# Constant products in TensorE's waits, low halves kept in the ring, and a new order at four hand-overs

## The chip, the cores and the metric

The kernel runs on one core of a Trainium2 chip. The metric is the device time of one execution in microseconds (us). A core has five engines that run their own instruction streams and wait for each other through semaphores: TensorE (PE in the profile; PEld are its weight loads), VectorE (DVE), ScalarE (ACT), GpSimd (POOL) and SyncE (SP), which here only issues DMAs.

## What is computed

One inference step of a hybrid backbone with two layers, on 128 context tokens and 256 latent tokens of width 1024 (384 tokens together). Cut to what matters:

```python
def _layer(x, mod, lp, router_w, router_b, rope, ctx_kv, h0):
    sh1, sc1, g1, sh2, sc2, g2 = mod          # Linear(SiLU(cond)), 6 x 1024 columns
    h = _rmsnorm(x, lp['norm1']) * (1 + sc1) + sh1
    q, k, v, xr, gr, ga, gb = jnp.split(h @ lp['w_in'], IN_SPLITS, axis=-1)
    att = ...                                 # grouped-query attention, 8 heads, 2 kv heads
    rnn, h_last = _rglru_bidir(xr, lp, h0)    # conv, gates, two scans
    merged = (jax.nn.sigmoid(ga) * (att @ lp['w_attn_proj'])
              + jax.nn.sigmoid(gb) * ((jax.nn.gelu(gr) * rnn) @ lp['w_rnn_proj']))
    x = x + g1 * (merged @ lp['w_out'])
    h2 = _rmsnorm(x, lp['norm2']) * (1 + sc2) + sh2
    x = x + g2 * _moe(h2, router_w, router_b, lp['w_gate_up'], lp['w_down'])
    return x, k, v, h_last
```

`_moe` routes each token to 2 of 16 experts (SwiGLU, inner width 512). After the second layer there is a last RMSNorm. All is fp32.

## The kernel before

**Precision.** Most products are made from two halves in the faster fp32r type: a high half (the rounded value) and a low half (value minus high half). ScalarE makes the high half of a weight tile (`high_part`, line 1031; `piece_high`, line 1226), VectorE the low half (`low_part`, line 1497; `piece_low`, line 1838), and TensorE adds high x high, high x low and low x high (`split_product`, line 522; `split_piece`, lines 820 and 826).

**Weights.** SyncE streams them in an order fixed by `chunk_order`. Chunks of 2 MB (1024 rows x 512 columns) go into a `ring` of three slots; the experts' pieces of 1 MB go into eight `spots`, six of which lie over the ring and two over `parts`. Before each load SyncE waits for the release of what was in the place (`released`): for a chunk whose products are split that is the last low half made of it. SyncE's queue is in order. Split products in order are q, xr, gr (the first 24, `EARLY`), then ap, rp, wo (the late 24); each has 8 column tiles of 128, four to a chunk. High and low halves of a tile go into one of three pairs of places (`w_parts`); for the late ones these lie in `hT`, `spare` and `xc`. `AHEAD` is 2: the halves of tile n + 2 are asked for when product n is due.

**The order in a layer.** TensorE: h products for k, v (`product`, line 511); split products q and xr; 24 attention units, each with scores, a product of gr, ga or gb, the turn of the probabilities, the two gate products of one recurrent pair from unit 8 on, and `attend` (line 685) of the unit before; then ap, rp, wo; squares for the norm; the router's logits (line 744); transposes of the rows (line 752); `rank` (line 772), `ids` (line 779), the gates (line 784); the turn of the first expert's rows (`xturn`, line 792) and 16 experts, each with four pieces of gate-up and two of down. ScalarE and VectorE follow the order of their own streams, written out by hand:

- End of attention. In unit 23 ScalarE runs `exps`, `lru_root(14)`, the tanh of gb, `pt_copy(23)`, `lru_tables(15)` (lines 1124 to 1134), `att_copy(22)` (line 1110), and behind the loop `lru_root(15)` (line 1140), `high_part(24)`, `att_copy(23)`, `high_part(25)`. VectorE runs `one_minus_square(15)`, `low_part(24)`, `att_split(7)`, `low_part(25)`, `scan(15)`. The last `attend` waits for `att_copy(22)`; product ap0 waits for its low half and `att_split(7)`.
- Experts. The results of experts 0 to 13 are stored to memory (`store_y`, line 1255) and gathered by token by GpSimd (line 1997) into `yg`; those of 14 and 15 are held on the chip and spread by a selection matrix (line 895). ScalarE scales the rows (line 1266), VectorE combines them (line 1893) and makes the low halves of the held ones (line 1888); TensorE transposes the rows (`rows_in`, line 890), adds the held ones, and VectorE adds the sums to x (`add_group`, line 1901, semaphore `group_added`).
- `one_more`. A branch that each engine takes by the number of further blocks (0 with these inputs) follows; the count is read by `value_load`. ScalarE asks for the Sqrt table by a one-column activation (line 1297) ahead of it.
- Into the next layer. SyncE issues kv, q0 and ada4 of layer 1 when the gathers are back. ScalarE squares x (line 1327), TensorE sums the squares with a matrix of ones (line 548), ScalarE takes the root (line 1005), VectorE the reciprocal (line 1461) and the product with x (line 1468), GpSimd (line 1965) and ScalarE (line 1041) apply the modulation, and product k0 starts. After layer 1 the rows are turned (line 951), squared (line 1332), rooted (line 1343), scaled (line 1947) and stored.

## Time and profile before

| | us |
|---|---|
| median of 3 runs (lowest, highest) | 1584.49 (1583.61, 1587.31) |
| the profiled execution, whole | 1587.41 |
| its span, first to last instruction | 1585.5 |
| TensorE busy | 1485.0 (94%) |
| VectorE busy | 1116.2 (70%) |
| ScalarE busy | 926.0 (58%) |
| mean granted TensorE clock | 0.967 |

Times in the rows are microseconds from the first instruction of the profiled execution. Busy time is the union of an engine's instructions. Matmul records overlap, their ends are modelled. The granted clock is 1.00 at 2.4 GHz and 0.50 at 1.2 GHz. What stands in square brackets at the end of a row is the idle time of the engine before it and what ended it; "issue" means that the profile shows no releaser.

### The profile page before, as it was taken

What the parts mean: (1) busy time and instruction counts of PE and PEld (TensorE: products, weight loads), DVE (VectorE), ACT (ScalarE), POOL (GpSimd) and SP (SyncE); (2) the same over time, 40 slices, a digit from 0 to 9 for tenths busy, and PEclk for the clock granted to TensorE, in tenths of its full rate; (3) what the DMA queues carried; (4) which work ended last, traced back from release to release, by engine and by line L of the source; (5) the groups of instructions that cost most, each with busy time, mean ns of one, the idle gap of its engine ahead of it and who ended that gap; (6) DMA issues with size and microseconds to landing.
All of it is one profiled execution on the core that took longest, in us unless ns stands there. A gap on an engine that the chain in (4) does not pass through costs nothing.

```text
span 1585.5 us, 19352 instructions
## 1 busy us (share of the span) xinstructions
PE 1485.0 (94%) x7317; PEld 1195.4 (75%) x7317; DVE 1116.2 (70%) x1709; ACT 926.0 (58%) x1174; POOL 153.3 (10%) x209
## 2 busy tenths in 40 slices
PE   6999999989996999999979999999899599999996
PEld 3699866669875788888748998665898378888885
DVE  4447656765646999999852665776564689999996
ACT  1333579962224877778742245899321467787874
POOL 0100012200010000000230000221000200000002
PEclk8999999989997999999989999999899699999999
DMA  9455422124656999999744554112340789999993
GB/s 349 163 199 203 153 103 101 62 102 166 212 193 253 358 406 408 409 408 404 278 162 154 186 199 161 62 62 90 128 160 1 279 311 407 413 411 410 408 357 121
DMA packets 132708, 373.01 MB, mean 235 GB/s; under 512 B 9216, under 2 KB 12672, under 8 KB 132608
## 3 DMA queue, kind: packets, MB, share of 16 engines
q1 hardware_dynamic: 113728, 326.57, 54.9%
q0 software_dynamic: 10432, 25.18, 4.5%
q10 hardware_dynamic: 8448, 19.94, 3.2%
q8 instruction: 63, 1.03, 0.3%
q14 instruction: 37, 0.30, 0.1%
HBM read 351.71 MB, written 19.94 MB: 234 GB/s over the span
## 4 chain that ended last, share of the span: by engine, by line
PE 79%; DVE 7%; ACT 4%; issue 4%; DMA 4%; POOL 1%; SPq 0%; POOLq 0%; DVEq 0%; ACTq 0%
PE bank L522 24%; PE bank L820 19%; PE bank L511 10%; PE bank L826 10%; PE bank L532 2%; PE bank L712 2%; PE bank L792 2%; DMA ring<-in_w_ada 1%; PE bank L685 1%; PE bank L548 1%; DMA expert_rows<-gb 1%; PE bank L541 1%; PE bank L622 1%; PE bank L617 1%; DMA tmp<-expert_rows,posu 1%
## 5 line engine op out<-in xcount | busy, mean ns | idle before, releaser
L1838 DVE TENSOR_TENSOR spot_low<-spot,piece_high 128x2048 fp32r<-128x2048 f32 x192 | 434.1, 2287 | 32.8 <-ACT piece_high L1226 31.5
L1226 ACT ACTIVATE piece_high<-spot 128x2048 fp32r<-128x2048 f32 x192 | 366.9, 1917 | 46.6 <-PE bank L826 45.4
L820 PE MATMUL bank<-piece_high,ga_r 128*128 128x512 f32 x768 | 310.9, 405 | 4.7 <-ACT ga_r L1231 2.2
L820 PE MATMUL bank<-spot_low,ga_r 128*128 128x512 f32 x768 | 303.7, 395 | 0.0
L826 PE MATMUL bank<-piece_high,ga_r 128*128 128x512 f32 x768 | 211.6, 397 | 0.0
L511 PE MATMUL bank<-hT,ring 128*128 128x384 f32 x576 | 198.0, 499 | 9.6 <-ACT hT L1041 6.5
L522 PE MATMUL bank<-parts_r,ga_r 128*128 128x384 f32 x768 | 202.6, 345 | 0.0
L820 PEld LDWEIGHTS bank<-piece_high,ga_r 128*128 128x128 f32 x768 | 145.6, 190 | 39.0 <-ACT ga_r L1231 3.0
L511 PEld LDWEIGHTS bank<-hT,ring 128*128 128x128 f32 x576 | 109.2, 195 | 82.6 <-issue 11.3
L826 PEld LDWEIGHTS bank<-piece_high,ga_r 128*128 128x128 f32 x768 | 145.1, 189 | 34.8
L820 PEld LDWEIGHTS bank<-spot_low,ga_r 128*128 128x128 f32 x768 | 145.9, 190 | 31.0
L522 PEld LDWEIGHTS bank<-parts_r,ga_r 128*128 128x128 f32 x768 | 138.3, 188 | 5.9 <-issue 5.0
L522 PE MATMUL bank<-parts_r,gb_r 128*128 128x384 f32 x384 | 129.7, 338 | 0.0
L522 PE MATMUL bank<-parts_r,hT_r 128*128 128x384 f32 x432 | 99.0, 356 | 9.1 <-DVE parts_r L1489 9.1
L522 PEld LDWEIGHTS bank<-parts_r,hT_r 128*128 128x128 f32 x432 | 81.3, 199 | 12.8 <-DVE parts_r L1489 10.9
L1497 DVE TENSOR_TENSOR gb_r<-ring,ga_r 128x1024 fp32r<-128x1024 f32 x48 | 58.5, 1222 | 44.1 <-ACT ga_r L1031 42.4
L1984 POOL DMA_INDIRECT gr<-h_rows,ids x32 | 44.0, 1375 | 464.0 <-PE bank L792 429.7
L1977 POOL DMA_DIRECT2D gatew<-in_lru_wa x64 | 34.2, 539 | 473.5 <-PE bank L712 473.5
L1031 ACT ACTIVATE hT_r<-ring 128x1024 fp32r<-128x1024 f32 x32 | 33.9, 1058 | 78.0 <-PE bank L522 78.0
L522 PEld LDWEIGHTS bank<-parts_r,gb_r 128*128 128x128 f32 x384 | 72.1, 188 | 0.0
L1001 ACT ACTIVATE tmp<-bank 128x512 f32<-128x512 f32 x24 | 14.3, 598 | 75.9 <-PE bank L532 75.9
L1965 POOL TENSOR_SCALAR hT<-hT,modA,modT 128x128 f32<-128x128 f32 x32 | 23.4, 745 | 361.6 <-DVE hT L1468 322.4
(308 smaller groups left out, 2289.3 us busy)
## 6 DMA issues: line engine op xcount, KB each, us to landing
spot<-in_w_gate_up SPq DMA_DIRECT2D x128, 1024.0 KB, 8.0
spot<-in_w_down SPq DMA_DIRECT2D x64, 1024.0 KB, 8.3
ring<-in_w_ada SPq DMA_DIRECT2D x24, 2048.0 KB, 8.0
ring<-in_w_in SPq DMA_DIRECT2D x22, 2048.0 KB, 8.0
expert_rows<-gb ACTq DMA_DIRECT2D x28, 512.0 KB, 7.3
ring<-in_w_attn_proj SPq DMA_DIRECT2D x4, 2048.0 KB, 8.6
ring<-in_w_rnn_proj SPq DMA_DIRECT2D x4, 2048.0 KB, 8.3
ring<-in_w_out SPq DMA_DIRECT2D x4, 2048.0 KB, 8.0
```

What stands on the lines that cost most here:

```text
L511: mm = pe.matmul(bank[:, 0:width], slot_kn(slot)[:, k, n * P:(n + 1) * P], rhs(k), start=(k == 0), stop=(k == KT - 1))
L522: mm = pe.matmul(bank[:, 0:T], w[:, k, :], x[:, k, :], start=(k == 0 and i == 0), stop=(k == KT - 1 and i == 2))
L532: mm = pe.matmul(bank[g:g + 32, :], cpad[:, k, :], slot_kn(s)[:, k, :], start=(k < 4), stop=(k >= 4), tile_position=(0, g))
L712: pe.matmul(bank[:, 0:CW], gatew[:, which, n % 2, :], xc[:, j, :], start=True, stop=True).then_inc(S("gemm_done"), 1)
L820: pe.matmul(out[n], high[:, 2 * q + k, :], w[:, k, n * 512:(n + 1) * 512], start=(q == 0 and k == 0 and i == 0), stop=False)
L826: mm = pe.matmul(out[n], low[:, 2 * q + k, :], w_high[:, k, n * 512:(n + 1) * 512], start=False, stop=(q == pieces - 1 and k == 1))
L1031: ac.activation(w_part(kind, n)[0], slot_kn(s)[:, :, n % 4 * P:(n % 4 + 1) * P], ACT.Copy)\
L1226: ac.activation(highs[p % HIGHS], spots[u], ACT.Copy).then_inc(S("piece_high"), 1)
L1497: ve.tensor_tensor(low, slot_kn(s)[:, :, n % 4 * P:(n % 4 + 1) * P], high.bitcast(F32), ALU.subtract)\
L1838: ve.tensor_tensor(spots_low[u], spots[u], highs[p % HIGHS].bitcast(F32), ALU.subtract)\
L1977: po.dma_start(gatew[half * 64:half * 64 + 64, which, n % 2, half * 64:half * 64 + 64], w[l, d, 2 * j + half]).then_inc(S(f"gatew_loaded{n ...
L1984: po.indirect_dma_start(out=dst, out_offset=None, in_=h2d[:, :], in_offset=bass.IndirectOffsetOnAxis(ap=idx, axis=0)).then_inc(sem, 16)
```

## The change

What it does, in the order of the diff:

1. High halves of late tiles go round four places (`late_high`: `spare` and three in `hT`), and their low halves are written over the tile itself in the ring slot (`w_low_part`). A late chunk is therefore released by its fourth product (`gemm_done`) and not by its last low half. `xc` is no longer a place for halves.
2. SyncE waits ahead of layer 1's kv chunk until all of layer 0's groups are added.
3. `run_on` gives TensorE products of `ident` and constants into a bank that nobody reads: two of 384 columns ahead of `rank`, four of 512 ahead of `ids`, three ahead of the first `xturn` and one behind it, three ahead of `rows_in`, six behind the square sums at the end of layer 0.
4. End of attention: `high_part(24)` goes behind `exps(23)`, and `lru_tables(15)`, `one_minus_square(15)` and `lru_root(15)` go behind `att_copy(23)` and the halves of tile 25.
5. In the last expert ScalarE copies and stores the result of expert 13 ahead of the last gate-up piece.
6. The activation that asks for the Sqrt table goes behind `one_more`.
7. VectorE makes the low halves of the held results between the combinations of rows and not behind them.

```diff
+LATE_HIGHS = 4
-        w_parts = [[(part(gaf_r, i), part(gbf_r, i)) for i in range(PAIRS_OF_PARTS)],
-                   [(part(hTf, 0), part(hTf, 1)), (part(hTf, 2), part(spare_r, 0)), (part(xcf, 0), part(xcf, 1))]]
+        w_parts = [(part(gaf_r, i), part(gbf_r, i)) for i in range(PAIRS_OF_PARTS)]
+        late_high = [part(spare_r, 0)] + [part(hTf, i) for i in range(LATE_HIGHS - 1)]
+        ring_r = sb_r("ring")
...
+        def w_high_part(kind, n):
             at = SPLIT_AT[kind, n]
+            return w_parts[at % PAIRS_OF_PARTS][0] if at < EARLY else late_high[at % LATE_HIGHS]
+        def w_low_part(l, kind, n):
+            at = SPLIT_AT[kind, n]
+            if at < EARLY:
+                return w_parts[at % PAIRS_OF_PARTS][1]
+            s = CHUNK_SLOT[CHUNK_AT[(l, f"{kind}{n // 4}")]][0]
+            return ring_r[:, s, :].rearrange("p (k n) -> p k n", k=KT)[:, :, n % 4 * P:(n % 4 + 1) * P]
...
-                if g[1:] in SPLIT_AT:
+                if SPLIT_AT.get(g[1:], EARLY) < EARLY:
                     return S("w_low"), split_no(*g) + 1
...
+                if l and name == "kv":
+                    sy.wait_ge(S("group_added"), l * KT)
...
+            def run_on(bank, times, width=512):
+                for _ in range(times):
+                    pe.matmul(bank[:, 0:width], ident, con[:, 256:256 + width], start=True, stop=True)
...
+                run_on(SB[1], 2, T)
                 bank = t_take((l, "rank", 0))
...
+                run_on(SB[1], 4)
                 bank = t_take((l, "ids", 0))
...
+                run_on(SB[1], 3)
                 xturn(0)
+                run_on(SB[1], 1)
...
+                run_on(G[2], 3)
                 for g in range(6):
                     rows_in(g)
...
                     mm.then_inc(S("ss_done"), 1)
+                    run_on(G[2], 6)
                     continue
...
-                    nth = at % EARLY
-                    if nth >= PAIRS_OF_PARTS:
+                    if at >= EARLY + LATE_HIGHS:
+                        ac.wait_ge(S("gemm_done"), G_AT[(l, *SPLIT[at - LATE_HIGHS])] + 1)
+                    elif at > EARLY:
+                        ac.wait_ge(S("gemm_done"), G_AT[(l, "gb", KT - 1)] + 1)
+                    elif PAIRS_OF_PARTS <= at < EARLY:
                         ac.wait_ge(S("gemm_done"), G_AT[(l, *SPLIT[at - PAIRS_OF_PARTS])] + 1)
-                    elif at >= EARLY:
-                        ac.wait_ge(S("gemm_done"), G_AT[(l, "gb", KT - 1)] + 1)
-                        if nth == 2:
-                            ac.wait_ge(S("lru_used"), (l + 1) * 16)
...
                     exps(i)
+                    if i == 3 * KT - 1:
+                        high_part(EARLY)
...
-                    if i >= KT:
+                    if KT <= i < 3 * KT - 1:
                         lru_tables(i - KT)
                     if i >= 1:
                         att_copy(i - 1)
-                lru_root(15)
-                high_part(EARLY)
                 att_copy(23)
                 high_part(EARLY + 1)
+                lru_tables(15)
+                lru_root(15)
...
-                    piece_high(f"gu{e}", 3)
+                    if e < NE - 1:
+                        piece_high(f"gu{e}", 3)
                     if e >= 2:
                         copy_y(e - 2)
+                    if e == NE - 1:
+                        store_y(e - 2)
+                        piece_high(f"gu{e}", 3)
...
-                ac.activation(smx[:, 0, 7:8], ones[:, 0:1], ACT.Sqrt)
...
                 one_more(0)
+                ac.activation(smx[:, 0, 7:8], ones[:, 0:1], ACT.Sqrt)
...
-                one_minus_square(15)
                 low_part(EARLY)
                 att_split(HEADS - 1)
                 low_part(EARLY + 1)
+                one_minus_square(15)
                 scan(15)
...
-                for i in range(HELD):
-                    ve.wait_ge(S("y_copied"), l * NE + SENT + i + 1)
-                    low_of(i, (SB_pair, G_pair)[i], slot_gate[:, SENT + i:SENT + i + 1]).then_inc(S("held_low"), 1)
+                    if t:
+                        i = t - 1
+                        ve.wait_ge(S("y_copied"), l * NE + SENT + i + 1)
+                        low_of(i, (SB_pair, G_pair)[i], slot_gate[:, SENT + i:SENT + i + 1]).then_inc(S("held_low"), 1)
```

## Rows read from the trace of the kernel before

**Rows 1.** The page: busy time by engine, and one of its costliest groups.

```profile
PE 1485.0 (94%) x7317; PEld 1195.4 (75%) x7317; DVE 1116.2 (70%) x1709; ACT 926.0 (58%) x1174; POOL 153.3 (10%) x209
...
L820 PE MATMUL bank<-spot_low,ga_r 128*128 128x512 f32 x768 | 303.7, 395 | 0.0
```

**Rows 2.** Windows: stretch, length, busy time of each engine, granted clock, DMA share, GB/s.

```profile
336.00:346.00 10.00, 6.32 (x21) 6.05 (x22) 7.19 (x15) 4.21 (x7) 0.00 (x0) 0.50 0.18 66
483.00:503.00 20.00, 11.58 (x39) 9.93 (x40) 14.32 (x27) 5.63 (x5) 2.96 (x3) 0.50 0.45 160
817.50:824.00 6.50, 5.43 (x9) 2.82 (x10) 5.48 (x8) 5.28 (x9) 6.50 (x6) 0.50 0.00 1
1251.00:1271.00 20.00, 9.84 (x43) 8.61 (x44) 14.75 (x40) 8.33 (x5) 2.97 (x3) 0.50 0.56 211
```

**Rows 3.** Timeline of TensorE in the routing: start, length, engine, line, operation.

```profile
487.29 1.42 PE L779 MATMUL bank<-gb_r 128*128 128x22 f32 x6 [5.48 <-DVE gb_r L1789]
...
494.31 1.97 PE L792 MATMUL bank<-con,gr 128*128 128x128 f32 x8 [3.02 <-DMA gr<-h_rows,ids]
497.39 0.79 PE L820 MATMUL bank<-piece_high,ga_r 128*128 128x512 f32 x1 [1.11 <-ACT ga_r L1231]
...
511.31 1.03 PE L792 MATMUL bank<-con,gr 128*128 128x128 f32 x8
...
1267.52 0.79 PE L820 MATMUL bank<-piece_high,ga_r 128*128 128x512 f32 x1 [1.11 <-ACT ga_r L1231]
```

**Rows 4.** Timeline of TensorE at the end of layer 0's attention.

```profile
336.49 1.20 PE L685 MATMUL bank<-pt,vl 128*128 128x128 f32 x4 [3.56 <-ACT qT L1110]
...
341.31 7.06 PE L522 MATMUL bank<-parts_r,hT_r 128*128 128x384 f32 x26 [3.19 <-DVE parts_r L1489]
```

**Rows 5.** Timeline of TensorE at the layers' ends and into layer 1.

```profile
795.98 0.41 PE L895 MATMUL bank<-qT_r,gb_r 128*128 128x384 f32 x1 [0.23 <-DVE gr_r L1888]
...
805.92 7.12 PE L548 MATMUL bank<-hT,ones 128*128 128x384 f32 x16 [3.42 <-issue]
818.57 13.33 PE L511 MATMUL bank<-hT,ring 128*128 128x384 f32 x32 [5.52 <-ACT hT L1041]
831.74 7.03 PE L617 MATMUL bank<-ring,hT 128*128 128x512 f32 x16
...
1572.27 2.84 PE L951 MATMUL bank<-con,xT 128*128 128x128 f32 x24 [0.58 <-issue]
```

**Rows 6.** Timeline of ScalarE at the end of layer 0's attention.

```profile
333.37 0.59 ACT L1124 ACTIVATE tmp<-bank,hb 128x387 f32<-128x387 f32 x1
...
336.09 0.26 ACT L1110 ACTIVATE qT<-bank 128x128 f32<-128x128 f32 x1
...
338.09 1.04 ACT L1031 ACTIVATE hT_r<-ring 128x1024 fp32r<-128x1024 f32 x1
339.04 0.26 ACT L1110 ACTIVATE qT<-bank 128x128 f32<-128x128 f32 x1
```

**Rows 7.** Timeline of VectorE, the last operation of scan(15).

```profile
346.38 0.56 DVE L1489 TENSOR_TENSOR gr_r<-gr,qT_r 128x384 fp32r<-128x384 f32 x1
```

**Rows 8.** The tile ring, issued between 790 and 792 us: kv and q0.

```profile
DMA to landing us min/median/max: 8.0/11.0/13.9
```

**Rows 9.** DMA queues between 803.2 and 804 us, and between 1569.7 and 1570.

```profile
q1 hardware_dynamic: 154, 0.29, 96.0%
q8 instruction: 1, 0.02, 8.2%
...
q8 instruction: 1, 0.02, 20.9%
```

**Rows 10.** Timeline of GpSimd, the modulation of the context tokens in layer 1.

```profile
816.93 8.07 POOL L1965 TENSOR_SCALAR hT<-hT,modA,modT 128x128 f32<-128x128 f32 x8 [30.07 <-DVE hT L1468]
```

**Rows 11.** Waits of TensorE over the span: us in total, times, longest.

```profile
PE bank L890 <- DVE tmp L1893: 4.0, 2, 2.0
```

**Rows 12.** Timeline of ScalarE at the end of layer 1.

```profile
1576.69 1.28 ACT L1343 ACT_TABLE_LOAD   x1
...
1578.19 0.58 ACT L1332 ACTIVATE hT<-bank 128x512 f32<-128x512 f32 x1
```

10 lines of the change are left out of this document (4 added, 6 removed).

## The prediction

> **What bounds the kernel now.** I read the page first: TensorE is busy for 94% of the span [rows 1], so a gain has to come out of its idle gaps or out of stretches in which its products run slowly. The table of windows gives the second kind: in three kinds of place the granted clock is at 0.50, the 1.2 GHz level [rows 2]: at the end of attention, in the routing, and on either side of the step from layer 0 to layer 1. Each of them follows a gap of TensorE. The reader should see in the timeline that the products of one and the same form take twice as long there: eight transposes 1.97 us against 1.03 [rows 3]. So a gap is paid twice, once as a wait and once as slow products behind it, and I went through the gaps with the timeline of each engine and the chain of waits. They are: the end of attention, 3.56 and 3.19 us [rows 4]; the routing, waits until 487.29, 494.31 and 497.39 us [rows 3]; the end of a layer, until 805.92 and 818.57 us [rows 5].
>
> **The change, part by part.**
>
> **1. End of attention, twice.** Before the last `attend`, TensorE waits for `att_copy(22)` at 336.09 us, which ScalarE issues behind `lru_tables(15)`; that takes from 333.37 to 336.09, 2.72 us [rows 6]. The change moves `lru_tables(15)` behind, and puts `high_part(24)`, 1.04 us [rows 6], ahead. So `att_copy(22)` starts at 336.09 - 2.72 + 1.04 = 334.41, and the last `attend` 1.68 us earlier, at 334.8. It takes 1.6 us, 1.20 of them in its first group of products [rows 4], the cached values behind it. `att_copy(23)` no longer stands behind `lru_root(15)` and `high_part(24)`: it comes at 336.45 in place of 339.04 [rows 6]. VectorE then needs only `att_split(7)`, two operations of about 1 us together, so product ap0 starts at about 337.75 and not at 341.31 [rows 4]: 3.5 us. What is late next is the low half for ap2: in VectorE's queue it stands behind `scan(15)`, which now ends near 346.5 (it was 346.94 [rows 7], and its root comes later relative to ap0). That half would be ready near 347.7. ap0 and ap1 still run partly at 0.50, since TensorE is idle here for over 3 us all the same, and ap1 ends after 348, so nothing waits; were the clock up, ap2 would wait and the gain would stop at about 4.3. I take 3.5 for each layer, 7.0 in all, bounds 6 and 8.6.
>
> **2. High halves in four places, low halves in the ring.** The weight slot is now free when the fourth product of a chunk is done and not when its low half is made, some 8 us (two products) later. A chunk lands 8.0 us after its issue when nothing is ahead of it [rows 8], and the products that need it come more than that later; SyncE's queue is in order, but the chunks behind wait for modulation products anyway. I cost it at nothing; if the cover were gone it would be up to 8 us at each of five chunks, which is the bound I do not take.
>
> **3. Constant products in the routing, twice.** One 512-column product costs 7.03 / 8 = 0.88 us at the full clock [rows 5], a 384-column one about three quarters, 0.66. Two of the latter go ahead of `rank`, four of 0.88 (3.5 us) ahead of `ids`, three (2.6 us) ahead of the turn of the first rows, one behind. `ids` starts at 487.29 after 5.48 us of idling, the turn after 3.02, gate-up after 1.11 [rows 3]: each fits while the clock is up. What they give: `ids` costs 1.42 us at the low level, so 0.7 less, of which 0.6 reaches the gather; the turn 1.97 down to 1.03, 0.9 less; and from 497.39 to the end of the low stretch at 503, 5.6 us at half rate, 2.8 less [rows 2, 3]. Layer 0: 4.3 us. In layer 1 the first piece starts at 1267.52 and the low stretch ends at 1271 [rows 2, 3], 1.8 us in place of 2.8: 3.3 us. Sum 7.6 us. The bounds are 8.5 and, should the dummies start at the low level, about -3 (the second rival). What hides behind: VectorE needs 4.5 us for the first two low halves and they begin earlier too.
>
> **4. Layer 0 to layer 1.** (a) Between the last product of the layer, 802.5, and the first square sum at 805.92 the profile names no releaser for 3.42 us [rows 5]. There stands the branch of `one_more`. An instruction transfer of 16 KB starts between 803.2 and 804, in a stretch that the three weight chunks issued from 791.1 on fill; in layer 1 the same branch costs 0.58 us [rows 5], and the like transfer starts between 1569.7 and 1570 with nothing else moving [rows 9]. TensorE goes on some 2.4 us after either. So I read the 3.42 as a code fetch behind 6 MB of weights. The change holds these loads back until `group_added` is complete, one addition after TensorE's last product, near 803.3, and TensorE has its code by then: the gap falls to 0.6, 2.8 us less. The squares, 7.12 us at a clock that falls on the way [rows 5], take 8 x 0.65 = 5.2 at the full one: 1.9 less. (b) The chunks now land 8.0 us and more after 803.4, kv at 811.5, where its first product comes at 813.8 at the earliest; q0 and ada4 (in the row the second of two lands after 13.9 us [rows 8]) are needed only some 12 us after that product. SyncE has nothing else queued behind. No cost. (c) Six dummies, 5.3 us, stand in the wait of 5.52 us for the normalised rows [rows 5]: they fit, and the first product runs at the full clock. GpSimd paces it, though: its eight pieces end at 825.0 [rows 10], so that of the time lost at the low level only about 1.2 us comes back. (a) and (c): 6.0 us, bounds 2.5 and 6.5.
>
> **5. Rows of the experts, twice.** `store_y(13)` goes ahead of one high half, so the rows may come back earlier; one low half of the held experts slips into the wait for the last rows. Together they could take away the idle 2.0 us ahead of the transposes [rows 11] and the 0.23 ahead of the spread at 795.98 [rows 5]. But three dummies, 2.6 us, now stand in that place, and TensorE runs them whatever has arrived. The transposes then start 0.5 us later, 0.2 of it stood as the wait ahead of the spread, and pauses between the two may hold some more: I cost the whole at 0.1 us lost, twice, bounds -0.3 and 0.6. Here the change gives back what it gained.
>
> **6. ScalarE's table for Sqrt.** It is asked for behind the branch and not ahead of it. In layer 1 a table load of 1.28 us stands at 1576.69, in series with the end, and after the Sqrt behind it Square runs at 1578.19 with no load of its own [rows 12]: one table serves both, and the load comes only because the branch hides which one is in. Behind the branch it is loaded in ScalarE's wait: 1.3 us less; everything behind it is in series. In layer 0 the load is hidden. The Trainium skill, page "ScalarE: Activation LUTs", section "What ACT_TABLE_LOAD costs", puts a switch at some 2.7 us with a drain; the Square at 1578.19, with the Sqrt before it, starts 1.5 us after the load does, so the trace does not agree; by the page the sum would be 1.4 us lower.
>
> **The sum.** 7.0 + 7.6 + 6.0 + 1.3 - 0.2 = 21.7 us. The profiled execution took 1587.4 us with a span of 1585.5, so it would take 1565.7. The median of the runs shown, 1584.5, is 2.9 below it: 1562.8, rounded to 1563.
>
> **The rivals.** First, the gap at 802.5 is the price of the taken branch itself and not of the loads. Against it: 0.58 us in layer 1. For it: layer 1 may have had its code by chance of position, and the change shifts positions. Then the 3.4 us and the slow squares stay: 1563 + 4.7 = 1568. The Trainium skill, page "Runtime: NRT & Kernel Launch", section "Instruction fetch mechanics", states such a rule: a taken branch whose target is not held stalls until the code is fetched. The trace agrees that there is a fetch, and leaves open what its length hangs on. Second, the dummies do not keep the clock up in the routing. For it: gaps of nearly 2 us remain between them, and `ids` and the gates have only 22 columns. Then the four ahead of `ids` last 7.0 us and end 1.6 late, the three ahead of the turn 5.3 and end 3.6 late in all, the one behind it adds 0.6; what follows has the full clock, 2.8 back. That is 1.4 lost for each layer in place of 3.8 gained: 1563 + 10.4 = 1573. It is also the case in which the change does not do what it says. Third, slower than before: low halves in the ring slot make the 48 late products slower, by TensorE reading weights from the slot that VectorE writes next to. The price is 48 times what each grows by; it decides from 25 / 48 = 0.5 us, a ninth of a product. Against it: the expert stage does the same in place, and its products on fresh low halves take 395 ns with no idling before them [rows 1]. With 0.6 us each the kernel would take about 1592.
>
> **How the numbers follow.** My forecast has 0.62, with a range of its own from 1558 to 1568. The branch has 0.14, the clock 0.18, the slower products 0.03, and 0.03 is left for small mishaps that eat everything. The range from 1558 (all upper bounds) to 1573 takes in the first three, but for the tails. A measurement here tells 0.2%, 3 us, from no change. Faster by more: 0.94; within: 0.03; slower: 0.03.
>
> **What would show it.** ap0 should start some 3.5 us earlier against the last `attend` but one; the granted clock should read 1.00 when gate-up begins, in both layers; the gap before the square sums should be under 1 us and the squares 5.2 us; the spread should start no earlier than now against the last down product; no table load at the second Sqrt. Wrong would be a wait of TensorE behind a run of dummies, a first product of layer 1 that waits for `ring`, or products of ap, rp and wo above 4.2 us.

## The result and the profile after

The changed kernel takes 1566.58 us (median of four executions, 1566.03 to 1567.22), where the kernel before takes 1584.05 (1583.37 to 1587.31): a ratio of 0.9886, 95% interval 0.9869 to 0.9903. The profiled execution took 1566.03 us with a span of 1564.2. The forecast was 1563, so it was 3.6 us too low, inside its range. One execution of this study, of the kernel without constant products in the routing, ran in a slow state (1888.3 us at a mean granted clock of 0.744) and is left out of its median.

Table of windows of the changed kernel; the columns are those of [rows 2].

```profile
334.00:340.00 6.00, 5.26 (x16) 5.27 (x17) 3.58 (x7) 5.94 (x9) 0.00 (x0) 0.50 0.25 89
484.00:487.00 3.00, 3.00 (x5) 1.12 (x4) 3.00 (x2) 0.00 (x0) 2.47 (x2) 0.50 0.52 173
487.40:800.00 312.60, 308.17 (x1428) 248.91 (x1427) 276.65 (x212) 232.68 (x171) 29.86 (x20) 1.00 0.95 367
800.00:1217.00 417.00, 402.16 (x2039) 325.15 (x2038) 249.73 (x532) 209.34 (x385) 41.67 (x72) 1.00 0.35 124
```

The column ahead of the DMA share, the granted clock, tells the story: of the 20 us at 0.50 in each routing [rows 2] about 3.4 are left, and between 487 and 1217 us the clock doesn't fall at all, neither at the step between the layers nor at the end of layer 1's attention. TensorE's timeline at the places of [rows 3], [rows 4] and [rows 5]:

```profile
332.48 0.68 PE L702 MATMUL bank<-pt,vl 128*128 128x128 f32 x4 [1.78 <-ACT qT L1132]
334.74 1.01 PE L539 MATMUL bank<-parts_r,spare_r 128*128 128x384 f32 x2 [1.35 <-DVE parts_r L1517]
...
481.36 0.81 PE L798 MATMUL bank<-gb_r 128*128 128x22 f32 x6 [1.95 <-DVE gb_r L1817]
...
483.36 4.52 PE L514 MATMUL bank<-con 128*128 128x512 f32 x6
487.72 1.04 PE L811 MATMUL bank<-con,gr 128*128 128x128 f32 x8
...
489.87 0.50 PE L839 MATMUL bank<-piece_high,ga_r 128*128 128x512 f32 x1 [0.25 <-ACT ga_r L1255]
...
784.76 0.30 PE L911 MATMUL bank<-con,gb 128*128 128x128 f32 x1 [0.75 <-DVE tmp L1921]
...
794.14 5.43 PE L565 MATMUL bank<-hT,ones 128*128 128x384 f32 x16 [0.93 <-ACT hT L1355]
799.41 5.31 PE L514 MATMUL bank<-con 128*128 128x512 f32 x12
805.10 0.88 PE L528 MATMUL bank<-hT,ring 128*128 128x384 f32 x2 [0.37 <-ACT hT L1063]
806.39 3.30 PE L528 MATMUL bank<-hT,ring 128*128 128x384 f32 x8 [0.41 <-POOL hT L1994]
810.70 7.36 PE L528 MATMUL bank<-hT,ring 128*128 128x384 f32 x22 [1.01 <-POOL hT L1994]
```

L514 is `run_on`, the constant products. The wait ahead of the last `attend` went from 3.56 to 1.78 us and the one ahead of ap0 from 3.19 to 1.35 [rows 4]; the idle time ahead of the square sums from 3.42 to 0.93 (what ends it now is a square of ScalarE, L1355), and the squares from 7.12 to 5.43 us [rows 5]; the turn from 1.97 to 1.04 [rows 3].

To see where the time went I subtract the start of the same instruction in the two profiled executions, place by place; what the difference grows by in a stretch is what that stretch gave. The sum is the 21.3 us between the two spans.

| stretch | forecast | layer 0 | layer 1 |
|---|---|---|---|
| up to the first query projection of layer 0 | 0 | 2.2 | |
| from there to ap2 (attention and its end) | 3.5 each | 4.0 | 5.7 |
| late products, up to the logits' end | 0 | -0.3 | -0.1 |
| routing, up to the first activation turn | 4.3 and 3.3 | 4.3 | 2.5 |
| last activation turn to the spread (rows) | -0.1 each | -0.9 | -1.4 |
| spread's end to layer 1's first query projection | 6.0 | 4.5 | |
| spread's end to the end | 1.3 | | 0.9 |

"Spread's end" here and below is the start of its last product. Two things must be known to read the table. The first row is not the change's: what is done up to there is the same, and the first query projection starts between 68.2 and 71.3 us in the profiles of this study (the kernel before, 70.75), with the clock low in other stretches of the first 50 us each time. And the profiled execution of the kernel before was 3.4 us above its median while that of the changed one was 0.6 below: 21.3 less 3.4 and less 0.6 is about the 17.5 between the medians.

### The profile page after: what moved, and what is told of

It is laid out like the page before. It is cut to its first block, busy times and chain, and to the rows that moved or that the text cites. A ratio compares the mean times of both kernels' runs of the same rounds, so it can differ in the third digit from the quotient of the medians.

```text
span 1564.2 us, 19475 instructions
## 1 busy us (share of the span) xinstructions
PE 1496.1 (96%) x7381; PEld 1192.7 (76%) x7381; DVE 1115.0 (71%) x1709; ACT 919.3 (59%) x1170; POOL 157.8 (10%) x209
## 4 chain that ended last, share of the span: by engine, by line
PE 78%; DVE 7%; ACT 4%; DMA 4%; issue 4%; POOL 2%; SPq 0%; POOLq 0%; DVEq 0%; ACTq 0%
PE bank L539 23%; PE bank L839 19%; PE bank L528 10%; PE bank L845 10%; PE bank L549 2%; DMA ring<-in_w_ada 2%; PE bank L729 2%; PE bank L811 2%; PE bank L702 1%; PE bank L565 1%; DMA expert_rows<-gb 1%; PE bank L639 1%; PE bank L634 1%; PE bank L558 1%; DMA ring<-in_w_out 1%
## 5 line engine op out<-in xcount | busy, mean ns | idle before, releaser
L539 PE MATMUL bank<-parts_r,ring_r 128*128 128x384 f32 x256 | 86.8, 339 | 0.0
L539 PEld LDWEIGHTS bank<-parts_r,hT_r 128*128 128x128 f32 x384 | 69.3, 188 | 3.8 <-DVE ring_r L1525 1.4
L1053 ACT ACTIVATE hT_r<-ring 128x1024 fp32r<-128x1024 f32 x36 | 37.1, 1053 | 37.7 <-PE bank L539 37.7
## 6 DMA issues: line engine op xcount, KB each, us to landing
ring<-in_w_rnn_proj SPq DMA_DIRECT2D x4, 2048.0 KB, 10.3
```

Of the source, the lines that this page charges most:

```text
L539: mm = pe.matmul(bank[:, 0:T], w[:, k, :], x[:, k, :], start=(k == 0 and i == 0), stop=(k == KT - 1 and i == 2))
L1053: ac.activation(w_high_part(kind, n), slot_kn(s)[:, :, n % 4 * P:(n % 4 + 1) * P], ACT.Copy)\
```

## The experiments

Executions of one and the same kernel lie up to 7 us apart here (the kernel before, 1580.92 to 1588.11 in one session). Between the profiles of the study the clock falls or doesn't in half a dozen short waits, each worth 1 to 1.5 us, and that is the likely reason. The changed kernel and its variants ran in different sessions, in which the kernel before had medians from 1582.94 to 1584.36. So I read each edit first in its own stretch of the profile, and the median second. Each kernel has one profile.

### The step from layer 0 to layer 1

**Without SyncE's wait.**

```diff
-                if l and name == "kv":
-                    sy.wait_ge(S("group_added"), l * KT)
```

> The changed kernel without the wait that SyncE holds ahead of layer 1's first query chunk; all else as changed. Theory A (the idle time ahead of the square sums is the fetch of the branch's code, and its length hangs on the weight transfers that run beside it): the gap ahead of the square sums returns from 0.93 us to about 3.4, the granted clock falls behind it, the squares take about 7 us and not 5.43; from the last product of layer 0 to the first of layer 1 the kernel loses 2.5 to 4.5 us, and the whole takes about 1569 to 1571 us. Theory B (the branch has its own price, and the shorter gap comes from the position of the code): the gap stays below 1.5 us and the time at 1566.6.

Measured: 1571.57 us, ratio 0.9925 (0.9906 to 0.9944) to the kernel before. TensorE's timeline and the DMA queues in the idle time:

```profile
798.80 5.51 PE L563 MATMUL bank<-hT,ones 128*128 128x384 f32 x11 [3.38 <-issue]
804.52 1.88 PE L563 MATMUL bank<-hT,ones 128*128 128x384 f32 x5 [0.21 <-issue]
...
q1 hardware_dynamic: 728, 1.46, 103.3%
q8 instruction: 1, 0.02, 1.7%
```

The stretch from the spread's end to the first query projection takes 43.25 us, as in the kernel before (43.16), where the changed one takes 38.61: the wait alone is worth the whole 4.6 us. The median is 5.0 above the changed kernel's, 0.6 more than the upper end of A. The squares start at the full clock and fall into a stretch at 0.50 from 800.0 to 803.4 us. The queues show what is different: in the 3.8 us up to the squares the weights (q1) fill the sixteen engines, one instruction transfer (q8) between them. In the changed kernel the queues' view of the gap, from 792.9 to 795.0 us, holds two instruction transfers and no weights; one of them:

```profile
q8 instruction: 1, 0.02, 3.3%
```

Theory A holds; the first rival of the forecast (the branch's own price) falls, since both kernels take the same branch. The Trainium skill, page "Runtime: NRT & Kernel Launch", section "Instruction fetch mechanics", has a taken branch wait for the fetch of its page; that there is such a wait agrees, with at most 0.5 to 1.0 us of idling in the twelve other profiles that have SyncE's wait, and 3.4 where weights move.

**Without the six constant products.**

```diff
                     mm.then_inc(S("ss_done"), 1)
-                    run_on(G[2], 6)
```

> The changed kernel without the six constant products in the wait for layer 1's first normalised rows. Theory A (GpSimd's pieces pace the first product, so that the clock there is worth little): the first product starts at the low level and the kernel loses 0.3 to 1.0 us: 1567 to 1567.6. Theory B (my forecast's term, 1.2 us, and the key and value product behind it also at the low level): 1567.8 or more. Theory C (the six end later than the rows are there): it gains up to 0.4 us.

Measured: 1564.72 us, 0.9883 (0.9860 to 0.9906).

```profile
805.81 5.30 PE L528 MATMUL bank<-hT,ring 128*128 128x384 f32 x10 [5.53 <-ACT hT L1062]
811.41 7.36 PE L528 MATMUL bank<-hT,ring 128*128 128x384 f32 x22 [0.30 <-POOL hT L1993]
...
804.17 8.05 POOL L1993 TENSOR_SCALAR hT<-hT,modA,modT 128x128 f32<-128x128 f32 x8 [25.14 <-DVE hT L1495]
```

The first ten products now run at 0.50, 5.30 us for what took 3.30 + 0.88 with waits of 0.41 and 1.01 between; and the key and value product behind them starts 14.44 us after GpSimd's first piece, exactly as in the changed kernel. So the six are worth nothing here: GpSimd's eight pieces, 8.05 us, set the pace at either clock. From the spread's end to the first query projection it takes 38.14 us; the other kernels with SyncE's wait take 38.15 to 38.66. All three theories gave them some price and all three were wrong in size; the idea of A (GpSimd paces it) holds, with 0 in place of 0.3 to 1.0. That the median is 1.9 us below the changed kernel's I don't count: the profiled execution was 1.0 above that of the changed kernel.

### The rows of the experts

**The old order of the store.**

```diff
-                    if e < NE - 1:
-                        piece_high(f"gu{e}", 3)
+                    piece_high(f"gu{e}", 3)
                     if e >= 2:
                         copy_y(e - 2)
-                    if e == NE - 1:
-                        store_y(e - 2)
-                        piece_high(f"gu{e}", 3)
                     if e >= 1:
                         piece_high(f"dn{e - 1}", 0)
-                    if 2 <= e < NE - 1:
+                    if e >= 2:
                         store_y(e - 2)
```

> The changed kernel with the old order of the store of the last but two expert's rows (one high half ahead of it again). Theory A (the last rows come late because GpSimd's gather calls start some 0.4 us later against VectorE's large operations and one of them then waits for such an operation's end; the earlier store runs under weight transfers and lands no earlier): the last gathered rows land 1 to 2 us earlier against the first turn of the rows, and the stretch from the last turn to the spread takes up to that much less in both layers: 1564.5 to 1566. Theory B (the dummies ahead of the rows set the start of the transposes, as my forecast said): nothing changes or it loses 0.2 us; 1566.6. The third case, the earlier store does help: the rows land 1.8 us later, 1568 or more.

Measured: 1564.61 us, 0.9885 (0.9865 to 0.9906). From the last activation turn to the spread it takes 11.41 and 11.43 us; the changed kernel takes 12.36 and 12.94, the kernel before 11.48 and 11.54. So with the old order 2.4 us less are spent here in the two layers. GpSimd's six calls that gather the rows back, and VectorE beside them, in layer 0 of the changed kernel (start, length):

```profile
766.42 2.76 POOL L2026 DMA_INDIRECT hT<-expert_rows,posu  x1 [49.37 <-issue]
...
771.98 2.49 POOL L2026 DMA_INDIRECT qT<-expert_rows,posu  x1 [0.30 <-issue]
774.77 1.89 POOL L2026 DMA_INDIRECT tmp<-expert_rows,posu  x1 [0.30 <-issue]
776.97 0.94 POOL L2026 DMA_INDIRECT tmp<-expert_rows,posu  x1 [0.30 <-issue]
...
761.67 6.70 DVE L1866 TENSOR_TENSOR spot_low<-spot,piece_high 128x2048 fp32r<-128x2048 f32 x3 [1.84 <-ACT piece_high L1250]
...
771.36 4.50 DVE L1866 TENSOR_TENSOR spot_low<-spot,piece_high 128x2048 fp32r<-128x2048 f32 x2 [0.40 <-ACT piece_high L1250]
```

and of this run:

```profile
764.20 1.03 POOL L2022 DMA_INDIRECT hT<-expert_rows,posu  x1 [47.92 <-issue]
765.53 2.15 POOL L2022 DMA_INDIRECT gb<-expert_rows,posu  x1 [0.30 <-issue]
...
770.47 0.94 POOL L2022 DMA_INDIRECT tmp<-expert_rows,posu  x1 [0.30 <-issue]
771.71 1.98 POOL L2022 DMA_INDIRECT tmp<-expert_rows,posu  x1 [0.31 <-issue]
```

A call that VectorE leaves alone takes 0.94 us. One that meets a low half, 2.29 us on VectorE, ends 0.81 us after that low half does: in the changed kernel the first at 769.18 (the third low half of the group ends at 768.37) and the fourth at 774.47 (VectorE's operation ends at 773.66). The changed order makes the high half of `gu15.3` later; its low half and the two behind it now run in one block, and the third ends 0.7 us later against the last turn. So the first call ends 0.7 us later too (-5.1 us, not -5.9), and the fourth, which had slipped in just ahead of the next low half, is caught by it. The sixth then ends 3.6 us behind the last turn, one place later than the 2.4 of the kernel before. (In this run it ends 0.15 us behind in layer 0 and 2.35 in layer 1; the constant products hold the spread at 11.4 either way.)

The earlier issue gave nothing back: against the last turn the store is issued at -15.0 in place of -13.2 us, and lands at -8.6 (6.4 us later) in place of -9.0 (4.2 later), while weight transfers still run.

The new order does not cost this every time. The first call starts 0.7 us after the last store has landed. Of the 16 layers profiled with the new order and whole low halves, in 13 the store lands 8.9 us or less ahead of the last turn, the third low half catches the first call, and the sixth ends 3.6 us behind the turn. In the other three (both layers of the kernel with two constant products ahead of the turn, further down, and layer 0 of the one without any in the routing) it landed 9.1 to 10.0 us ahead: the first call started 8.4 to 9.3 us ahead and was over before the third low half could hold it up, the sixth ended at 2.35, and the spread started at 11.4 as with the old order. One of them, the first two calls, 7.3 and 5.1 us ahead of the turn at their ends:

```profile
766.51 1.19 POOL L2026 DMA_INDIRECT hT<-expert_rows,posu  x1 [48.73 <-issue]
768.01 1.90 POOL L2026 DMA_INDIRECT gb<-expert_rows,posu  x1 [0.30 <-issue]
```

In none of the six layers with the old order and whole low halves did a sixth call end later than 2.4. The cost of the order is thus 0.9 to 2.0 us in a layer where the store lands too late for the first call to be over before the third low half, as in 13 of 16, and nothing in the others.

**The low halves in two.** This tests the mechanism by itself, with the new order kept.

```diff
-                    ve.tensor_tensor(spots_low[u], spots[u], highs[p % HIGHS].bitcast(F32), ALU.subtract)\
-                        .then_inc(S("piece_low"), 1)
+                    if name in (f"dn{NE - 2}", f"gu{NE - 1}", f"dn{NE - 1}"):
+                        ve.tensor_tensor(spots_low[u][:, 0:1024], spots[u][:, 0:1024],
+                                         highs[p % HIGHS].bitcast(F32)[:, 0:1024], ALU.subtract)
...
```

> The changed kernel with the low halves of the last weight chunks of the expert stage (the last one of gate-up of the last expert, and those of the last two down projections) made by VectorE as two operations of 128x1024 each in place of one of 128x2048. Theory A (a row-gather call of GpSimd that meets a running low-half operation completes only 0.8 us after that operation ends): the calls that stand beside them shrink from 2.5 and 1.9 us to 1 to 1.9 us, the sixth call ends 1 us or more earlier against the first turn of the rows than the 3.59 us of the changed kernel, and the stretch to the spread gives back up to 1 us in each layer: 1564.6 to 1566. Theory B (the calls are long for a reason of their own, such as the descriptors or the transfers): the calls keep their times and nothing changes, 1566.6.

Measured: 1565.09 us, 0.9887 (0.9863 to 0.9910); last turn to spread 11.41 us in both layers.

```profile
772.43 0.94 POOL L2033 DMA_INDIRECT tmp<-expert_rows,posu  x1 [0.30 <-issue]
773.67 1.11 POOL L2033 DMA_INDIRECT tmp<-expert_rows,posu  x1 [0.30 <-issue]
...
772.74 1.23 DVE L1867 TENSOR_TENSOR spot_low<-spot,piece_high 128x1024 fp32r<-128x1024 f32 x1 [0.40 <-ACT piece_high L1250]
```

The sixth call meets the first half operation (until 773.97) and ends at 774.78, again 0.81 us after it; it takes 1.11 us. In layer 1 it ends 1.35 us after the last turn and not 3.6. Theory A holds: what a gather call waits for is the end of VectorE's operation, whether that takes 2.29 or 1.23 us. The Trainium skill, page "SBUF — State Buffer", section "SBUF: two separate sides", has a rule that fits: VectorE, with two operands in SBUF, and GpSimd share a pair of ports that one holds for a whole instruction. The calls' waits fit it. That the lock is held for a whole instruction does not show on VectorE's side: its next low half starts right behind the one that a call waited for and keeps its 2.29 us while that call runs. No run shows that it is this pair of ports and nothing else that they wait for.

**Without the three constant products ahead of the rows.**

```diff
-                run_on(G[2], 3)
                 for g in range(6):
                     rows_in(g)
```

> The changed kernel without the three constant products ahead of the transposes of the experts' rows. Theory A (the rows themselves are late, the dummies stand in a wait that is there anyway): 1566.6 within 0.5 us, with the transposes starting no earlier; if the clock falls in that gap, up to 1 us more for each layer. Theory B (my forecast: the dummies are what the transposes wait for): the transposes start 0.5 us earlier or more in each layer, 1565 to 1565.6.

Measured: 1570.60 us, 0.9912 (0.9889 to 0.9935). TensorE's first transpose of layer 0, and the window behind it:

```profile
787.68 0.45 PE L911 MATMUL bank<-con,gb 128*128 128x128 f32 x1 [3.38 <-DVE tmp L1920]
...
787.50:790.50 3.00, 2.82 (x14) 2.85 (x15) 1.23 (x2) 1.23 (x2) 0.00 (x0) 0.50 1.02 398
```

TensorE idles 3.38 us in layer 0 and 2.76 in layer 1, the clock falls behind both, and from the last turn to the spread it takes 13.86 and 13.04 us (12.36 and 12.94 in the changed kernel, whose last rows in layer 1 landed 1.1 us later). The transposes start 2.6 us after the last rows have landed in all four of these layers, with the dummies (landed 7.81 us after the last turn, start at 10.44) and without (7.86 and 10.49). In the changed kernel, then, the rows are what is late and the dummies cost nothing, as A has it with its price for the clock; my forecast's reason (they are what the transposes wait for) is wrong for the kernel as it is. The median is 4.0 us above the changed kernel's and A allowed 2.5: the stretches hold 1.6, and the profiled execution lost 2.8 more before layer 0's first query projection and 1.5 behind the wait for layer 1's wo0, where the clock fell.

**The same with the rows on time:** the old order of the store and no dummies.

> The changed kernel with the old order of the last store of rows and without the three constant products ahead of the transposes of these rows. Theory A (with the rows on time the dummies, 2.7 us, are what the transposes wait for, as my forecast priced them): the spread starts earlier against the last turn than the 11.41 us of the run with the old order and the dummies, by up to 0.6 us in each layer. Theory B (with the rows on time TensorE's wait is over 2 us with or without them, and the clock falls or not by chance): the spread starts at 11.41 to 11.5 us, or 1 to 1.5 later in a layer in which the clock falls. Time: 1563.5 to 1564.6 by A, 1564.6 to 1567 by B.

Measured: 1564.53 us, 0.9874 (0.9850 to 0.9898); last turn to spread 10.69 and 10.24 us, where the old order with the dummies has 11.41 and 11.43.

```profile
785.71 0.30 PE L911 MATMUL bank<-con,gb 128*128 128x128 f32 x1 [1.66 <-DVE tmp L1916]
...
1542.62 0.30 PE L911 MATMUL bank<-con,gb 128*128 128x128 f32 x1 [1.19 <-DVE tmp L1916]
```

So with the rows on time the dummies do hold the transposes back, by 0.7 and 1.2 us, and behind the waits without them, 1.66 and 1.19 us, the clock did not fall. Both readings were right, each in its own case. Layer 0 also bears on the moved low half of the held experts: 10.69 us against 11.48 in the kernel before, with the same order of the store. 0.3 of this is that the last rows landed 0.3 us earlier; from the first transpose to the spread it takes 1.91 in place of 2.39 us, and that 0.5 is what the moved low half can be worth. It was not undone alone.

**Old order and short low halves.**

> The changed kernel with two repairs: the old order of the last store of rows, and the low halves of the last chunks in two operations each. If both act on the same thing (the time of the sixth gather call against VectorE's low halves), they do not add: each alone brought the spread to 11.41 us after the last turn, and so do both: 2.4 us less than the changed kernel in the two layers, 1564.2, with the sixth call ended before 1.4 us after the last turn in both layers. If they add, the spread starts before 11.2 us and the time is 1563.5 or less.

Measured: 1566.37 us, 0.9888 (0.9864 to 0.9912), last turn to spread 11.41 us in both layers: they do not add, as one would think of two remedies for one thing; TensorE's dummies are the next limit. The time itself is 2 us above what I gave. In the profile the 2.4 us are there; 2.0 are lost ahead of layer 0's first query projection and 1.3 at the end of layer 1's attention, where the clock fell for 6.8 us in this execution and not in the changed kernel's.

**All three repairs.**

> The changed kernel with three repairs: the old order of the last store of rows, the low halves of the last chunks in two operations each, and no constant products ahead of the transposes of the rows. Theory A (the rows come on time by the first two, and the dummies are then what the transposes wait for): the spread starts 10.2 to 10.7 us after the last turn in both layers, where the changed kernel has 12.36 and 12.94, so 4.0 to 4.9 us less in the two layers and a time of 1561.7 to 1562.6. Theory B (the clock falls in the wait without the dummies, as it did once in the run that had only them taken out): 1 to 1.5 us of that is lost again in one layer or both, 1562.6 to 1565.

Measured: 1561.72 us (1560.32 to 1564.32), 0.9865 (0.9847 to 0.9883), last turn to spread 10.24 us in both layers, 2.1 and 2.7 less than in the changed kernel.

```profile
773.84 1.97 POOL L2028 DMA_INDIRECT tmp<-expert_rows,posu  x1 [0.30 <-issue]
...
782.78 0.30 PE L911 MATMUL bank<-con,gb 128*128 128x128 f32 x1 [1.20 <-DVE tmp L1923]
```

Theory A holds. The sixth call ends 1.35 us behind the last turn. The kernel's slowest execution is faster than the fastest of the changed kernel; the medians are 4.9 us apart, and the stretches of the rows 4.8. Measured each against the kernel before in its own session, the two differ by less, 0.9865 to 0.9886 (3.3 us), and the intervals overlap.

### The routing

**No constant products in the routing.**

```diff
-                run_on(SB[1], 2, T)       # ahead of rank
-                run_on(SB[1], 4)          # ahead of ids
-                run_on(SB[1], 3)          # ahead of the turn
-                run_on(SB[1], 1)          # behind it
```

> The changed kernel without the constant products in the routing (two ahead of the rank, four ahead of the ids, three ahead of the first turn, one behind it); the others stay. Theory A (they keep the clock up for gate-up behind them): the granted clock is at 0.50 at the start of gate-up again, and the kernel loses about what their place gained, 4.3 us in layer 0 and 2.5 in layer 1: 1572 to 1574. Theory B (they run while TensorE would wait and the clock comes back by itself at about the same time): within 1 us of 1566.6. In layer 1, where three of them ran at the low level and ended 0.85 us after the rows had landed, I expect the loss to be the smaller one.

Measured: 1571.21 us (median of three executions, 1567.74 to 1572.91), 0.9930 (0.9907 to 0.9954).

```profile
480.73 1.43 PE L796 MATMUL bank<-gb_r 128*128 128x22 f32 x6 [5.46 <-DVE gb_r L1813]
487.06 1.97 PE L809 MATMUL bank<-con,gr 128*128 128x128 f32 x8 [2.32 <-DMA gr<-h_rows,ids]
490.14 0.79 PE L837 MATMUL bank<-piece_high,ga_r 128*128 128x512 f32 x1 [1.11 <-ACT ga_r L1251]
...
474.00:493.00 19.00, 9.22 (x42) 8.09 (x43) 13.72 (x38) 8.06 (x5) 2.95 (x3) 0.50 0.58 213
```

The long stretch at 0.50 is back, and so are the waits of [rows 3], but for the one for the gathered rows, 2.32 us in place of 3.02. From the ids to the first activation turn it takes 24.6 and 24.2 us; the changed kernel takes 22.04 in both layers. So the dummies are worth 2.6 and 2.2 us here, 4.8 together, where theory A had 6.8. The profiled execution is nevertheless only 1.7 us above that of the changed kernel: layer 0's end of attention took 1.4 us less and its rows 0.9 less than there. In 21 of the 22 layers of the kernels with all of these products this stretch takes 22.0 to 22.3 us; in one (short low halves, layer 0) the clock was at 0.50 for 6.8 us and it took 23.7. The kernel before takes 26.3 and 24.55: of layer 0's 4.3 us 1.7 come without any dummy. 0.7 of these are the shorter wait for the gathered rows; the rest is where the low stretch lies: it ends 3.7 us after gate-up's start here and 5.9 after it in the kernel before. Nothing in the edit accounts for that, so I take it for chance; a second profile could divide the 4.3 otherwise.

**Two in place of three ahead of the turn.** In the changed kernel these three run at 0.50 in both layers and, with the gates' end, last 4.52 us. In layer 0 the rows land as they end; in layer 1 they last until 0.9 us behind the rows' landing.

```diff
-                run_on(SB[1], 3)
+                run_on(SB[1], 2)
```

> The changed kernel with two and not three constant products ahead of the first turn of the gathered rows. Theory A (in layer 1 they run at the low level and end 0.85 us after the rows have landed): layer 1 gains about 0.8 us there and layer 0 neither gains nor loses over 0.3, as there the rows land when the dummies end; 1565.8. Theory B (the third one is what brings the clock back before the turn): the turn and the start of gate-up run at 0.50 in one layer or both and cost 1 to 3 us: 1567.5 to 1570.

Measured: 1566.51 us, 0.9901 (0.9878 to 0.9924).

```profile
487.30 1.97 PE L811 MATMUL bank<-con,gr 128*128 128x128 f32 x8 [0.98 <-DMA gr<-h_rows,ids]
...
1247.09 0.50 PE L839 MATMUL bank<-piece_high,ga_r 128*128 128x512 f32 x1 [0.25 <-ACT ga_r L1255]
```

Each theory holds in one layer: layer 0 idles 0.98 us, its turn runs at 0.50 and it loses 0.95 us up to the first activation turn; layer 1 gains 0.6. The sum is close to nothing, and so is the median's change. This is the kernel in which the rows of the experts came on time in both layers with the new order of the store.

### The end of attention

**The old order.**

```diff
                     exps(i)
-                    if i == 3 * KT - 1:
-                        high_part(EARLY)
...
+                lru_root(15)
+                high_part(EARLY)
                 att_copy(23)
                 high_part(EARLY + 1)
-                lru_tables(15)
-                lru_root(15)
```

with `lru_tables(15)` ahead of `att_copy(22)` and `one_minus_square(15)` ahead of `low_part(24)` again.

> The changed kernel with the old order at the end of attention (tables and root of the last scan ahead of the high halves, on ScalarE and on VectorE). Theory A (that order alone holds attend and ap0 back): from the first query projection to ap2 each layer loses what it had gained, 4.0 us where the granted clock falls for 6.8 us in the changed kernel and 5.4 to 5.7 us where it falls shorter or not at all, together 9.4 to 11 us: 1576 to 1578. Theory B (part of that gain is the clock's, which falls now here and now there whatever the order): the loss is 7 us or less, as I forecast: 1573.6 or less.

Measured: 1575.39 us, 0.9951 (0.9936 to 0.9965), 8.8 us above the changed kernel.

```profile
340.41 1.01 PE L539 MATMUL bank<-parts_r,spare_r 128*128 128x384 f32 x2 [3.21 <-DVE parts_r L1515]
...
1106.88 1.01 PE L539 MATMUL bank<-parts_r,spare_r 128*128 128x384 f32 x2 [3.91 <-DVE parts_r L1515]
```

The waits of [rows 4] are back, the 3.57 us ahead of `attend` too. From the first query projection to ap2 it takes 281.5 and 280.2 us, the changed kernel 277.3 and 275.6: 4.2 and 4.7, 8.9 together. That is less than A's 9.4 and more than B's 7, and the median lies between the two as well; the order is the cause, and the clock moves its size: in layer 1 it fell for 6.8 us here and for 10.3 in the kernel before, which took 281.2 us, 1.0 more. The twelve profiled kernels that have the new order show how: 24 times the end of attention, 11 times with a stretch of 6.8 us at 0.50 and 276.9 to 277.5 us from projection to ap2, 13 times with 3.4 us or nothing and 275.6 to 276.0. Where the clock stays, ap2 waits for its low half, and that wait ends the gain:

```profile
1107.05 0.62 PE L539 MATMUL bank<-parts_r,hT_r 128*128 128x384 f32 x2 [1.13 <-DVE ring_r L1525]
```

### The end of the kernel

**The table's request ahead of the branch.**

```diff
+                ac.activation(smx[:, 0, 7:8], ones[:, 0:1], ACT.Sqrt)
                 one_more(0)
-                ac.activation(smx[:, 0, 7:8], ones[:, 0:1], ACT.Sqrt)
```

> The changed kernel with ScalarE's request of the Sqrt table ahead of the branch again. Theory A (a table load stands again in series with the end, as the branch hides which table is in): from the end of the last layer's spread to the end of the kernel 13.3 us become 14.2 to 14.6, 0.9 to 1.3 us lost: 1567.5 to 1567.9. Theory B (the gain at the end came from the shorter square and turn stage at another clock): no change, 1566.6.

Measured: 1568.64 us, 0.9909 (0.9883 to 0.9935); spread's end to the end 14.22 us, in the changed kernel 13.30. The load of [rows 12] stands there again:

```profile
1556.05 1.28 ACT L1371 ACT_TABLE_LOAD   x1
1557.35 0.29 ACT L1371 ACTIVATE rt<-rt 128x1 f32<-128x1 f32 x1
```

and the changed kernel has none ahead of its first Sqrt:

```profile
1556.68 0.29 ACT L1371 ACTIVATE rt<-rt 128x1 f32<-128x1 f32 x1
```

The other kernels with the request behind the branch take 12.8 to 13.3 us for this stretch, so it is worth 0.9 to 1.4. Theory A holds. The median's 2.1 us are more than A's 0.9 to 1.3; where the rest was lost the profile, which was of the fastest execution, does not show.

## Why the prediction was right, and where its steps were wrong

**1. End of attention: the mechanism right, the term too small.** 3.5 each against 4.0 and 5.7. The waits shrank as worked out, by 1.78 and 1.84 us in layer 0, 3.6 together. What failed is the clock: ap0 starts 4.4 us earlier against the first query projection, because the last `attend` now runs at 1.00 (0.68 us, 1.20 in [rows 4]); and the sentence that ap0 and ap1 "still run partly at 0.50" because TensorE idles over 3 us holds only at times. It idles in two parts, 1.78 and 1.35 us, and in 13 of 24 cases the clock falls briefly or not at all behind them. My cap of 4.3 was too low as well: in layer 1 ap2 waits 1.13 us for its low half and starts 9.8 us behind ap0, which is where I had it (9.95), but ap0 itself is 0.9 earlier than I had it. Of layer 1's 5.7 us, 4.7 are the order's by the run that undid it; the other 1.0 is the longer low stretch of the kernel before.

**2. High halves, and low halves in the ring: nearly nothing, as costed.** The products of ap, rp and wo kept their 4.2 us (from ap2 to the last wo it takes 108.6 and 104.6 us, before 108.4 and 104.6), so the rival of slower products is out; 0.3 and 0.1 us were lost in the whole stretch. This part was not undone alone.

**3. Routing: 7.6 forecast, 6.8 measured.** Layer 0's 4.3 came out to the tenth, but partly by luck: 2.6 are the dummies', and 1.7 come without them, by the position of the low stretch, for which no run shows a reason, and a shorter wait for the gathered rows. In both layers the three ahead of the turn ran at 0.50, and in layer 1 they held the turn back 0.9 us; that is a piece of the second rival inside a case where the forecast holds, since the clock was up again for the turn and for gate-up.

**4. The step between the layers: 6.0 forecast, 4.5 measured.** (a) held: 2.8 + 1.9 forecast, 4.6 by taking the wait away. One detail was read wrongly from the diff: the wait stands behind the issue of kv, so that kv was on its way at 782.3 and only q0 and ada4, 4 MB, were held. The row takes two issues together, kv at its start and q0 at its end:

```profile
782.28 12.11 SPq L478 DMA_DIRECT2D ring<-in_w_in  x2
```

kv landed at 790.1. In the kernel before it had landed at 799.1 too, ahead of the gap, so that what filled the queues there was q0 and ada4 and not 6 MB. The wait cost nothing, as forecast. (c) is the term that was mis-sized: 1.2 us for the six dummies, measured 0. I had seen that GpSimd paces the product and still gave the clock a part of it.

**5. The rows: -0.2 forecast, -2.3 measured.** The failed step is "the rows may come back earlier; one low half ... could take away the idle". I priced the earlier store by its place in ScalarE's queue and never asked what the high half moved behind it delays. That was the 0.7 us of a low half, and behind it a gather call that waits for VectorE. The loss to allow for in this part should have been one place in GpSimd's queue, 1.24 us, in each layer; it came in 13 of 16 layers. The reason that I did give for a loss, that the dummies hold the transposes back, did not apply, since the rows were later still.

**6. The table: 1.3 against 0.9 (0.9 to 1.4 over the kernels that have it).** Right; the load was 1.28 us and is gone.

**The sum.** The terms of the change came to 19.1 us in the profiles, against 21.7: attention gave 2.7 more than its terms, the rows took 2.1 more, the step between the layers gave 1.5 less, the routing 0.8, the late products and the end 0.4 each. The start gave 2.2 that no term had, so that the forecast for the profiled execution, 1565.7, missed its 1566.0 by only 0.3; that closeness is luck, as errors of up to 2.7 us on both sides cancelled. Nearly all of the 3.6 us of the medians comes from the last step of the sum: I took off the 2.9 us by which the profiled execution of the kernel before stood above its median, as if the terms were the same in each. They are not. That execution lost time by the clock in its waits, ahead of the first query projection among others, and part of what I counted as the change's gain was this.

## What to carry to other kernels

When an instruction is moved ahead of another, price the other one too: what it feeds, and which instruction of a third engine will now stand beside it. Look at more than one profile before the price is believed: here the same order cost nothing in 3 of 16 layers. Constant products that keep the clock up paid only in waits behind which nothing else paces TensorE: in the routing they gave 2.6 and 2.2 us, ahead of a product that GpSimd paces 0, ahead of rows that come on time they cost 0.7 to 1.2. Hold weight loads back from a branch that has to fetch its code: here that was worth 4.6 us for one wait.

## What the runs showed of the hardware

- A gather call of GpSimd takes 0.94 us alone, and ends 0.81 us after the end of a VectorE operation (two operands in SBUF) that it meets, for operations of 2.29 and of 1.23 us. Calls that a whole operation caught took 1.0 to 3.0 us, those that a half one caught 1.0 to 2.0.
- The clock can fall or not behind one and the same wait: with the same 2.23 us wait of TensorE ahead of layer 1's wo0 it fell for 3.4 us in four of the fourteen profiles (each of a kernel of its own, with the same products here) and not in the others, and cost 1.5 us there. One of the four, and the changed kernel at the same place:

```profile
1175.00:1178.00 3.00, 3.00 (x10) 3.00 (x11) 0.91 (x1) 0.00 (x0) 0.00 (x0) 0.50 0.03 5
...
1175.00:1178.00 3.00, 3.00 (x19) 3.00 (x18) 0.22 (x1) 0.00 (x0) 0.00 (x0) 1.00 0.02 5
```

- A store of 512 KB that is issued 1.8 us earlier, under weight transfers, did not land earlier as a rule: 4.9 to 7.0 us to landing in the new place, 2.9 to 4.6 in the old, over all profiles. Against the last turn it landed between -10.2 and -8.0 us in the new place and between -10.4 and -8.6 in the old.
